# Expert pairs in alternating halves, a scatter that waits for the one two pairs ahead, and a reordered last pair

## The chip, the cores and the metric

The kernel runs on one core of a Trainium2 chip. The metric is the time of one execution on the device in microseconds (us); the profile gives beside it the span of the profiled execution, from its first to its last recorded event. Engines are called PE (TensorE), DVE (VectorE), ACT (ScalarE), POOL (GpSimd) and SP (SyncE); PEld is PE's loading of weights.

## The reference, cut to what matters

The whole is a transformer-like block of two parts on 512 tokens of width 1024. Only its last step is touched, a mixture of experts: 32 experts in 4 groups of 8; each token goes to one group and, in it, to its two best experts.

```python
g_sel = jnp.argmax(g_logits, axis=-1)
e_in = jnp.take_along_axis(e_logits, g_sel[:, None, None], axis=1)[:, 0]
top_v, top_i = lax.top_k(e_in, TOP_K_EXPERTS)
...
for g in range(N_GROUPS):
    a = jnp.einsum('nd,edf->nef', hf, w_gate[g])
    b = jnp.einsum('nd,edf->nef', hf, w_up[g])
    hid = jax.nn.silu(a) * b * gates[:, g, :, None].astype(hf.dtype)
    out = out + jnp.einsum('nef,efd->nd', hid, w_down[g])
```

So two experts of different groups never share a token, and two experts of one group often do. All is float32.

## The kernel before

**Pairs.** The experts are worked on in 16 pairs (`PAIRS`), each of the same expert number in two groups; 64 slots (`CAP`) for each expert, 128 rows in all. A list made from the routing (`listed`, columns of `ixg`) names the token of each slot; an empty slot names none and its row isn't moved. The order of the pairs is first all 8 of groups 0 and 1, then all 8 of groups 2 and 3 (`of_pairs`, and the same order in the arrays `w_gu` and `w_dn` that the host lays out). Neighbouring pairs are therefore of the same two groups.

**One pair u**, step by step:

1. POOL `gather(u)`: an indirect DMA fetches the pair's rows of `h_rows` (DRAM) into `hg[:, u % 2]` (`ex_rows` in the trace). It copies the list's column first (L2631) and issues at L2632.
2. PE `turn(u)` (L2721): 8 transposes of these rows. DVE `copy_rows(u)` (L2876, L2879) brings them into `hgT`.
3. PE `gate_up(u)` (L2734): 32 matmuls against two weight loads of 2 MB; after the first 16 `gu_half` counts, after all `gu_done`.
4. ACT `silu(u)` (L2841), DVE `hidden(u)` (L2886).
5. PE `turn_hidden(u)` (L2744), DVE `copy_hidden(u)` (L2891).
6. PE `down(u)` (L2757): 16 matmuls against one weight load of 2 MB, 8 into each of two banks of PSUM.
7. ACT `copy_y(u)` (L2846) and DVE `copy_y(u)` (L2896) bring one bank each into `ys[:, u % 2]`.
8. POOL `scatter(u)`: copies the list's column (L2639), waits for the two copies (L2641, L2643) and issues an indirect DMA that adds the rows to `out` (L2644).
9. POOL `y_is_out` (L2650, L2651): waits until a scatter has landed and gives its half of `ys` free (`y_free`).

**Order on PE.** The loop of `first_round` interleaves three pairs:

```python
for u in range(PAIRS):
    gate_up_first(u)
    if u + 1 < PAIRS:
        turn(u + 1, (u + 1) % 2, 16 * ((u + 1) // 2 + 1))
    if u:
        down_first(u - 1)
    turn_hidden(u, u % 2)
```

**Order on POOL.** Gathers and scatters are issued by one instruction stream that stands still at each wait, and both move on one DMA queue, q0 in the profile. Three gathers stand ahead, then `scatter(0)`, then a loop over `step`: gather, wait for the scatter of the pair before, scatter, and the same for the other half of the buffers. Since the scatters add to the same DRAM rows, no scatter is issued before the last one has landed.

**Weights.** SP loads 48 parts of 2 MB (`PARTS`: two of gate and up, one of down for each pair) through 11 places in SBUF, in the order in which PE uses them; a part is issued when the one 11 ahead has been used. They move on queue q1. The first 11 are loaded while the routing is worked out.

If an expert has more than 64 tokens, further rounds follow; with these inputs they don't run.

Of the kernel before, what the change touches and what calls it, by code (L numbers as in the profile page):

```python
# [15 lines left out]
ALU = mybir.AluOpType  # L16
# [5 lines left out]
P = 128  # L22
# [120 lines left out]
class Core:  # L143


    def __init__(self, nc, ctx, dram):
        self.nc, self.ctx, self.dram = nc, ctx, dram
        self.names = 0
        self.scope, self.held = ExitStack(), []
        self.W = ctx.enter_context(nc.sbuf_tensor("weight_slots", [P, SLOTS, KT * P], F32))  # L150
        self.w_in = [ctx.enter_context(nc.semaphore(f"weight_slot_{j}")) for j in range(SLOTS)]
        self.w_n = [0] * SLOTS

        self.place_in = [ctx.enter_context(nc.semaphore(f"place_in_{i}")) for i in range(PLACES)]

    def sem(self, name):
# [73 lines left out]
    def load_down(self, sp, i, pair):  # L230
        src = self.dram["w_dn"][bass.ds(pair, 1)].rearrange("x p c -> p (x c)").rearrange("p (s c) -> p s c", c=KT * P)
        sp.dma_start(self.place(i), src).then_inc(self.place_in[i], 16)

    def load_part(self, sp, c):

        kind, u, h = PARTS[c]
        if kind == "g":
            self.load_gate_up(sp, c % PLACES, u, h)
        else:
            self.load_down(sp, c % PLACES, u)  # L240

# [2049 lines left out]
def routing_programs(core, lot, omT, x_rows, gate, most, ixg, hg, hg_in, out):  # L2291
# [58 lines left out]
    def tensor(pe):  # L2350
# [40 lines left out]
        for j in range(2 * NB):  # L2391
            for x in range(2):
                units = of_pairs(unit_id[:, j], x)
                last = nc.tensor.matmul(pL[CAP * x:CAP * x + CAP, 0:PAIRS], at_slot[:, j], units, start=(j == 0),
                                        stop=(j == 2 * NB - 1))
        last.then_inc(listed, 1)
        pe.wait_ge(spread_rs, 2)
        for kind, table in enumerate((unit_one, unit_id)):
            for j in range(2 * NB):
                for x in range(2):  # L2400
                    last = nc.tensor.matmul(pz[CAP * x:CAP * x + CAP, kind * PAIRS:(kind + 1) * PAIRS], at_slot[:, j],  # L2401
                                            of_pairs(table[:, j], x), start=(j == 0), stop=(j == 2 * NB - 1))
        last.then_inc(listed_rs, 1)

# [160 lines left out]
def expert_programs(core, lot, most, ixg, hg, hg_in, out):  # L2565
# [10 lines left out]
    ix_ready, gu_half, gu_done, silu_done, th_done, d_done, more_spread, more_listed, more_ready = (  # L2576
        core.sem(n) for n in ("ix_ready", "gate_up_half", "gate_up", "silu", "hidden_turned", "down", "spread_rounds",
                              "listed_rounds", "rounds_ready"))
    t_done, ta_out, tb_out, hid_done, hT_done, ya, yb = (
        lot.t_done, lot.ta_out, lot.tb_out, lot.hid_done, lot.hT_done, lot.ya, lot.yb)  # L2580
# [44 lines left out]
    def gpsimd(pool):  # L2625
# [22 lines left out]

        def y_is_out(e, value):
            pool.wait_ge(y_out[e], value)  # L2650
            nc.gpsimd.tensor_tensor(ixc[:, 6:7], ixc[:, 2 + e:3 + e], ixc[:, 2 + e:3 + e], ALU.add).then_inc(y_free, 1)  # L2651

        def step(u, stored, ahead):
            if ahead:
# [10 lines left out]
            scatter(u + 1, 0)  # L2665
            chain.restart()

        def first_round():
            gather(1, 1)
            gather(2, 0)  # L2670
            gather(3, 1)
            pool.wait_ge(lot.x_stored, 16)
            scatter(0, 0)
            chain.restart()
            with pool.Fori(0, PAIRS // 2 - 2) as i:
                step(pool.snap(i * 2 + 1), pool.snap(i * 16 + 16), True)
            step(PAIRS - 3, first_out - 16, False)
            y_is_out(0, first_out)
            pool.wait_ge(y_free, PAIRS + 1)
            scatter(PAIRS - 1, 1)  # L2680
            chain.restart()

        def run(r):
            first, n = r * PAIRS, PAIRS
# [29 lines left out]
    def tensor(pe):  # L2714
# [31 lines left out]
            last.then_inc(th_done, 1)  # L2746

        def down(u, e, at, w):
            pe.wait_ge(place_in[at], w)
            pe.wait_ge(hT_done, u + 2)  # L2750
            pe.wait_ge(ya, u + 1)
            pe.wait_ge(yb, u + 1)
            for half in range(2):
                for f in range(FF // P):
                    for x in range(2):
                        rows = slice(CAP * x, CAP * x + CAP)
                        last = nc.tensor.matmul(pY[rows, half, :], hidT[:, e, f * P + CAP * x:f * P + CAP * x + CAP],  # L2757
                                                core.as_down(at)[:, x, f, half * 512:half * 512 + 512], start=(f == 0),
                                                stop=(f == FF // P - 1))
            last.then_inc(d_done, 1)  # L2760

        def filled_first(c):
            return 16 * (c // PLACES + 1)
# [7 lines left out]
            down(u, u % 2, c % PLACES, filled_first(c))  # L2771

        def first_round():
            for u in range(PAIRS):
                gate_up_first(u)
                if u + 1 < PAIRS:
                    turn(u + 1, (u + 1) % 2, 16 * ((u + 1) // 2 + 1))
                if u:
                    down_first(u - 1)
                turn_hidden(u, u % 2)  # L2780
            down_first(PAIRS - 1)

        def list_rounds():

            pe.wait_ge(more_spread, 2)
            for n, what in enumerate((slot_id, slot_rs, at_slot)):
                for j in range(2 * NB):
                    for x in range(2):
                        units = of_pairs(at_unit[:, j], x)
                        last = nc.tensor.matmul(pL[CAP * x:CAP * x + CAP, n * (MORE // 2):(n + 1) * (MORE // 2)], what[:, j],  # L2790
                                                units, start=(j == 0), stop=(j == 2 * NB - 1))
            last.then_inc(more_listed, 1)

# [43 lines left out]
    def scalar(act):  # L2837
# [3 lines left out]
            nc.scalar.activation(sa[:, e], pG[:, e, 0:FF], ACT.Silu, scale=rs2[:, e, 0:1]).then_inc(silu_done, 1)  # L2841

        def copy_y(u, e):
            act.wait_ge(d_done, u + 1)
            act.wait_ge(y_free, u + 1)
            nc.scalar.copy(ys[:, e, 0:512], pY[:, 0, :]).then_inc(ya, 1)  # L2846

# [20 lines left out]
    def vector(dve):  # L2868
# [29 lines left out]
        def run(r):  # L2898
            first, n = r * PAIRS, PAIRS
            hidden(first, 0)  # L2900
            copy_rows(first + 1, 1)
            copy_hidden(first, 0)
            with dve.Fori(0, n // 2 - 1) as i:
                u = dve.snap(i * 2 + (first + 1))
                hidden(u, 1)
                copy_rows(u + 1, 0)
                copy_y(u - 1, 0)
                copy_hidden(u, 1)
                hidden(u + 1, 0)
# [4 lines left out]
            hidden(u, 1)  # L2914
            copy_y(u - 1, 0)
            copy_hidden(u, 1)
            copy_y(u, 1)
            if not isinstance(r, int):
                copy_rows(u + 1, 0)
# [163 lines left out]
def layout(inputs):  # L3083
# [28 lines left out]
    arr["w_gu"] = np.ascontiguousarray(gu.reshape(2, 2, EPG, 2, KT // 2, P, 2 * FF).transpose(0, 2, 5, 3, 1, 4, 6)).reshape(  # L3112
        PAIRS, P, 2, -1)
    arr["w_dn"] = np.ascontiguousarray(dw.reshape(2, 2, EPG, FF // P, P, D).transpose(0, 2, 4, 1, 3, 5)).reshape(PAIRS, P, -1)
# [63 lines left out]
```

## Time and profile before

| | |
|---|---|
| three runs | 1533.16, 1533.18 and 1535.5 us, median 1533.18 |
| the profiled execution | 1533.7 us, its span 1531.9 us, mean granted clock 0.982 |
| busy in the span | PE 1418.7 us, DVE 820.9, ACT 418.4, POOL 56.4 |
| the experts | from the first gather at 1280.5 us to the end |

In rows of a timeline the columns are start and duration in us, engine, line of the kernel, operation, output and inputs, shapes and count; in brackets how long the engine was idle before it and what ended that. A duration of a matmul group covers its whole count. In rows of the chain they are start, duration and what the time went to. In windows: the stretch and its length, then the busy time of each engine with its number of instructions, the granted clock of PE (1.00 is 2.4 GHz, 0.50 is 1.2 GHz), the busy share of the 16 DMA engines and GB/s.

### The profile page before, as it was taken

What the parts mean: (1) busy time and instruction counts of PE and PEld (TensorE: products, weight loads), DVE (VectorE), ACT (ScalarE), POOL (GpSimd) and SP (SyncE); (2) the same over time, 40 slices, a digit from 0 to 9 for tenths busy, and PEclk for the clock granted to TensorE, in tenths of its full rate; (3) what the DMA queues carried; (4) which work ended last, traced back from release to release, by engine and by line L of the source; (5) the groups of instructions that cost most, each with busy time, mean ns of one, the idle gap of its engine ahead of it and who ended that gap; (6) DMA issues with size and microseconds to landing.
All of it is one profiled execution on the core that took longest, in us unless ns stands there. A gap on an engine that the chain in (4) does not pass through costs nothing. (4 is left out here: it accounts for less than half of the span.)

```text
span 1531.9 us, 14470 instructions
## 1 busy us (share of the span) xinstructions
PE 1418.7 (93%) x5162; PEld 760.5 (50%) x5162; DVE 820.9 (54%) x1808; ACT 418.4 (27%) x682; POOL 56.4 (4%) x114
## 2 busy tenths in 40 slices
PE   7999999999999999999989999998899795989875
PEld 3455555555555558888854344445444433333321
DVE  5567677676776847776443348965333414211210
ACT  2434444443345315101110133134301430000000
POOL 0000000000000000000000000000000001122211
PEclk9999999999999999999999999999999996999998
DMA  7131111321110114222342121002023468999994
GB/s 283 29 109 55 51 46 42 100 66 55 55 42 28 42 53 154 83 83 83 111 164 79 39 82 55 28 9 83 28 71 143 167 253 341 402 407 407 411 404 131
DMA packets 38056, 201.94 MB, mean 132 GB/s; under 512 B 6880, under 2 KB 8800, under 8 KB 31072
## 3 DMA queue, kind: packets, MB, share of 16 engines
q1 hardware_dynamic: 30688, 186.29, 32.4%
q0 software_dynamic: 4608, 8.40, 2.3%
q10 hardware_dynamic: 2688, 6.29, 1.1%
q8 instruction: 44, 0.72, 0.2%
q14 instruction: 28, 0.23, 0.0%
HBM read 196.77 MB, written 12.58 MB: 137 GB/s over the span
## 5 line engine op out<-in xcount | busy, mean ns | idle before, releaser
L446 PE MATMUL gla_proj<-hT,weight_slots 128*128 128x512 f32 x864 | 378.1, 592 | 1.9 <-DVE hT L809 1.9
L446 PEld LDWEIGHTS gla_proj<-hT,weight_slots 128*128 128x128 f32 x864 | 160.9, 190 | 188.8 <-issue 188.1
L2734 PE MATMUL moe_banks<-weight_slots,moe_room 128*64 128x512 f32 x400 | 91.4, 605 | 12.6 <-DMA weight_slots<-in_w_gu 9.7
L1503 PE MATMUL mid_p_proj<-hT,weight_slots 128*128 128x512 f32 x208 | 94.7, 603 | 2.4 <-DVE hT L1671 2.4
L2886 DVE SCALAR_TENSOR_TENSOR moe_room<-moe_banks,moe_kept,moe_room 128x256 f32<-128x256 f32 x16 | 7.7, 484 | 125.8 <-ACT moe_room L2841 118.8
L600 ACT ACTIVATE gla_level_decay<-gla_level_decay 128x1024 f32<-128x1024 f32 x56 | 59.0, 1057 | 39.4 <-DVE gla_level_decay L729 39.0
L1503 PEld LDWEIGHTS mid_p_proj<-hT,weight_slots 128*128 128x128 f32 x208 | 39.7, 193 | 53.9 <-issue 52.8
L2734 PEld LDWEIGHTS moe_banks<-weight_slots,moe_room 128*64 128x64 f32 x400 | 29.0, 139 | 66.6 <-issue 53.1
L1328 PE MATMUL rn_p_out<-mT,weight_slots 128*128 128x512 f32 x128 | 58.4, 618 | 3.4 <-PEq L949 3.4
L472 PEld LDWEIGHTS gla_level<-gla_level_q,gla_level_k 128*128 128x128 f32 x448 | 55.0, 192 | 11.5 <-issue 11.5
L564 ACT COPY gla_raw<-gla_proj 128x512 f32<-128x512 f32 x38 | 22.4, 590 | 130.6 <-PE gla_proj L446 130.6
L1328 PE MATMUL rn_p_out<-y2T,weight_slots 128*128 128x512 f32 x128 | 55.2, 593 | 1.5 <-PEq L170 1.5
L472 PE MATMUL gla_level<-gla_level_q,gla_level_k 128*128 128x128 f32 x448 | 56.3, 275 | 0.0
L446 PE MATMUL gla_proj<-weight_slots,hT 128*128 128x512 f32 x128 | 55.9, 592 | 0.0
L2451 POOL DMA_INDIRECT ex_rows<-h_rows,ix_rows x1 | 1.2, 1187 | 1280.1 <-issue 1280.1
L745 DVE COPY spare<-spare 128x1 f32<-128x1 f32 x64 | 9.6, 150 | 71.7 <-PE gla_level L472 71.1
L746 DVE COPY_PREDICATED gla_scores<-gla_level_masks,gla_level 128x512 f32<-128x512 int32 x64 | 46.8, 731 | 2.2
L2757 PE MATMUL moe_banks<-weight_slots,moe_room 128*64 128x512 f32 x176 | 41.9, 619 | 5.4 <-DMA weight_slots<-in_w_dn 4.6
L2841 ACT ACTIVATE moe_room<-moe_banks,moe_kept 128x256 f32<-128x256 f32 x16 | 7.6, 474 | 133.3 <-PE moe_banks L2734 133.3
L1328 PEld LDWEIGHTS rn_p_out<-mT,weight_slots 128*128 128x128 f32 x128 | 25.3, 199 | 35.4 <-issue 35.4
L1328 PEld LDWEIGHTS rn_p_out<-y2T,weight_slots 128*128 128x128 f32 x128 | 24.2, 190 | 31.8 <-issue 31.8
L446 PEld LDWEIGHTS gla_proj<-weight_slots,hT 128*128 128x128 f32 x128 | 23.9, 190 | 28.2 <-issue 28.2
(453 smaller groups left out, 2310.5 us busy)
## 6 DMA issues: line engine op xcount, KB each, us to landing
weight_slots<-in_w_gu SPq DMA_DIRECT2D x25, 2048.0 KB, 27.6
weight_slots<-in_w_dn SPq DMA_DIRECT2D x11, 2048.0 KB, 37.8
weight_slots<-in_w_gla SPq DMA_DIRECT2D x40, 512.0 KB, 3.6
weight_slots<-in_w_merge SPq DMA_DIRECT2D x32, 512.0 KB, 4.2
weight_slots<-in_w_out SPq DMA_DIRECT2D x16, 512.0 KB, 4.1
weight_slots<-in_w_v SPq DMA_DIRECT2D x3, 2048.0 KB, 7.8
hT<-in_w_gu SPq DMA_DIRECT2D x3, 2048.0 KB, 37.0
weight_slots<-in_w_u SPq DMA_DIRECT2D x8, 512.0 KB, 5.9
```

Of the source, the lines that this page charges most:

```text
L446: last = nc.tensor.matmul(pj[:, n % 2, :], lhsT, rhs, start=(k == 0), stop=(k == KT - 1))
L472: last = nc.tensor.matmul(pA[:, l % 2, c * P:(c + 1) * P], k, q, start=True, stop=True)
L564: nc.scalar.copy(dst, pj[:, n % 2, :]).then_inc(evac, 1)
L600: nc.scalar.activation(Tl[:, l % 2], Tl[:, l % 2], ACT.Exp).then_inc(e_ready, 1)
L745: chain(nc.vector.tensor_copy(core.spare[:, 1:2], core.spare[:, 0:1]))
L746: nc.vector.copy_predicated(A[:], masks[:, l].unsqueeze(1).to_broadcast([P, NB, P]), pA[:, l % 2].rearrange("p (n t) -> p n t", t=P)).then ...
L1328: last = nc.tensor.matmul(pp[:, j, :], core.slot(j)[:, k, :], src[:, k, :], start=(k == 0), stop=(k == KT - 1))
L1503: last = nc.tensor.matmul(pw[:, n % 2, :], a, b, start=(k == 0), stop=(k == KT - 1))
L2734: last = nc.tensor.matmul(pG[rows, e, :], hgT[:, k, rows], core.as_gate_up(at[k // 4])[:, x, k % 4, :], start=(k == 0), stop=(k == KT - 1))
L2757: last = nc.tensor.matmul(pY[rows, half, :], hidT[:, e, f * P + CAP * x:f * P + CAP * x + CAP], core.as_down(at)[:, x, f, half * 512:half ...
L2841: nc.scalar.activation(sa[:, e], pG[:, e, 0:FF], ACT.Silu, scale=rs2[:, e, 0:1]).then_inc(silu_done, 1)
L2886: nc.vector.scalar_tensor_tensor(out=hid[:, e], in0=pG[:, e, FF:2 * FF], scalar=rs2[:, e, 1:2], in1=sa[:, e], op0=ALU.mult, op1=ALU.mult). ...
```

## The change

It has six parts. (`step` stays as it is, for the further rounds; the last hunk of the diff is ACT's.)

1. `of_pairs`, `in_pairs` and the two host arrays: the pairs now alternate, pair 0 of groups 0 and 1, pair 1 of groups 2 and 3, and so on. Neighbouring pairs have no token in common.
2. `step_first` and `first_round` on POOL: a scatter waits only for the one two pairs ahead. `scatter(1)` stands directly behind `scatter(0)` and ahead of the loop, and the loop's scatters are one pair further on than its gathers were.
3. `down` gives two signals, `d_half` after the first bank and `d_done` after the second; ACT copies the first bank after `d_half`. Each half waits for its own bank to be free.
4. On PE `turn_hidden(15)` moves ahead of `down(14)`; on DVE `copy_hidden(15)` moves ahead of `copy_y(14)`.
5. The last weights (down of pair 15) come in two loads of 1 MB, by columns; the first half of `down(15)` waits for the first alone.
6. `y_is_out` reads the other index column.

```diff
 def of_pairs(units, x):
-    return units.rearrange("p (g x m) -> p x g m", x=2, m=EPG)[:, x]
+    return units.rearrange("p (r y x m) -> p x r m y", y=2, x=2, m=EPG)[:, x]
+def in_pairs(units):
+    return units.rearrange("p (r m y) -> p r m y", y=2, m=EPG)
...
+    def load_down_halves(self, sp, i, pair):
+        src = self.dram["w_dn"][pair].rearrange("p (x f c) -> p x f c", x=2, c=D)
+        for half, loaded in enumerate((self.last_half, self.place_in[i])):
+            cols = slice(half * 512, half * 512 + 512)
+            sp.dma_start(self.as_down(i)[:, :, :, cols], src[:, :, :, cols]).then_inc(loaded, 16)
...
         def y_is_out(e, value):
             pool.wait_ge(y_out[e], value)
-            nc.gpsimd.tensor_tensor(ixc[:, 6:7], ixc[:, 2 + e:3 + e], ixc[:, 2 + e:3 + e], ALU.add).then_inc(y_free, 1)
+            other = ixc[:, 3 - e:4 - e]
+            nc.gpsimd.tensor_tensor(ixc[:, 6:7], other, other, ALU.add).then_inc(y_free, 1)
 
         def step(u, stored, ahead):
             if ahead:
                 gather(u + 3, 0)
             y_is_out(0, stored)
             if not ahead:
                 pool.wait_ge(y_free, u + 2)
             scatter(u, 1)
             if ahead:
                 gather(u + 4, 1)
             y_is_out(1, stored)
             if not ahead:
                 pool.wait_ge(y_free, u + 3)
             scatter(u + 1, 0)
             chain.restart()
+        def step_first(u, stored, ahead):
+            if ahead:
+                gather(u + 3, 0)
+            y_is_out(0, stored)
+            if not ahead:
+                pool.wait_ge(y_free, u + 2)
+            scatter(u + 1, 0)
+            if ahead:
+                gather(u + 4, 1)
+            y_is_out(1, stored)
+            if not ahead:
+                pool.wait_ge(y_free, u + 3)
+            scatter(u + 2, 1)
+            chain.restart()
         def first_round():
             gather(1, 1)
             gather(2, 0)
             gather(3, 1)
             pool.wait_ge(lot.x_stored, 16)
             scatter(0, 0)
+            scatter(1, 1)
             chain.restart()
             with pool.Fori(0, PAIRS // 2 - 2) as i:
-                step(pool.snap(i * 2 + 1), pool.snap(i * 16 + 16), True)
-            step(PAIRS - 3, first_out - 16, False)
+                step_first(pool.snap(i * 2 + 1), pool.snap(i * 16 + 16), True)
+            step_first(PAIRS - 3, first_out - 16, False)
             y_is_out(0, first_out)
-            pool.wait_ge(y_free, PAIRS + 1)
-            scatter(PAIRS - 1, 1)
-            chain.restart()
...
         def down(u, e, at, w):
-            pe.wait_ge(place_in[at], w)
             pe.wait_ge(hT_done, u + 2)
-            pe.wait_ge(ya, u + 1)
-            pe.wait_ge(yb, u + 1)
             for half in range(2):
+                if half or isinstance(u, int) and u == PAIRS - 1:
+                    pe.wait_ge(place_in[at] if half else core.last_half, w if half else 16)
+                else:
+                    pe.wait_ge(place_in[at], w)
+                pe.wait_ge((ya, yb)[half], u + 1)
...
-            last.then_inc(d_done, 1)
+                last.then_inc((d_half, d_done)[half], 1)
...
         def first_round():
-            for u in range(PAIRS):
+            for u in range(PAIRS - 1):
                 gate_up_first(u)
-                if u + 1 < PAIRS:
-                    turn(u + 1, (u + 1) % 2, 16 * ((u + 1) // 2 + 1))
+                turn(u + 1, (u + 1) % 2, 16 * ((u + 1) // 2 + 1))
                 if u:
                     down_first(u - 1)
                 turn_hidden(u, u % 2)
+            gate_up_first(PAIRS - 1)
+            turn_hidden(PAIRS - 1, (PAIRS - 1) % 2)
+            down_first(PAIRS - 2)
             down_first(PAIRS - 1)
...
         def copy_y(u, e):
-            act.wait_ge(d_done, u + 1)
+            act.wait_ge(d_half, u + 1)
```

**How the order moves on POOL.** Around the entry to the loop, the kernel before has `gather(3)`, `scatter(0)`, then the loop's first piece, `gather(4)`:

```order
L2632 DMA ex_rows<-h_rows,ex_ix 128x1024
L2639 COPY ex_ix<-ix_rows 128x1
L2641 ISA
L2641 TENSOR_TENSOR ex_ix<-ex_ix 128x1
L2643 TENSOR_TENSOR ex_ix<-ex_ix 128x1
L2644 DMA out<-moe_room,ex_ix 512x1024
L134 ISA
L2675 UNCONDITIONAL_BRANCH
L2675 ISA
L2631 ISA
L2631 COPY ex_ix<-ix_rows 128x1
L2632 DMA ex_rows<-h_rows,ex_ix 128x1024
```

The changed kernel, at the same place, from the end of `scatter(0)` to `gather(4)` (its lines are some 15 further on):

```order
L2658 TENSOR_TENSOR ex_ix<-ex_ix 128x1
L2659 DMA out<-moe_room,ex_ix 512x1024
L2654 COPY ex_ix<-ix_rows 128x1
L2656 TENSOR_TENSOR ex_ix<-ex_ix 128x1
L2658 TENSOR_TENSOR ex_ix<-ex_ix 128x1
L2659 DMA out<-moe_room,ex_ix 512x1024
L134 ISA
L2707 UNCONDITIONAL_BRANCH
L2707 ISA
L2646 ISA
L2646 COPY ex_ix<-ix_rows 128x1
L2647 DMA ex_rows<-h_rows,ex_ix 128x1024
```

`gather(4)` stood behind one scatter and stands behind two; as the loop keeps this distance, every gather from the fourth on moves from behind `scatter(u - 4)` to behind `scatter(u - 3)`.

**On PE**, the end of the experts; before, from `turn_hidden(14)` and `gate_up(15)` on:

```order
L2744 MATMUL moe_banks<-ident,moe_room 128x128 x2
L2734 MATMUL moe_banks<-weight_slots,moe_room 64x512 x16
L2757 MATMUL moe_banks<-weight_slots,moe_room 64x512 x8
L2744 MATMUL moe_banks<-ident,moe_room 128x128 x2
L2757 MATMUL moe_banks<-weight_slots,moe_room 64x512 x8
```

And in the changed kernel, from `down(13)` on:

```order
L2788 MATMUL moe_banks<-x_rows,moe_room 64x512 x8
L2773 MATMUL moe_banks<-ident,moe_room 128x128 x2
L2763 MATMUL moe_banks<-weight_slots,moe_room 64x512 x16
L2773 MATMUL moe_banks<-ident,moe_room 128x128 x2
L2788 MATMUL moe_banks<-weight_slots,moe_room 64x512 x16
```

The second `turn_hidden` (that of pair 15) has moved ahead of `down(14)`, so that the two last `down` stand together.

## Rows read from the trace of the kernel before

**Rows 1.** The page, DMA queues: packets, MB, share of 16 engines' span.
```profile
q0 software_dynamic: 4608, 8.40, 2.3%
```

**Rows 2.** Windows of the experts' stage, 100 us each.
```profile
1300.00:1400.00 100.00, 92.45 (x438) 33.85 (x438) 20.88 (x44) 7.42 (x14) 24.56 (x48) 0.98 1.01 406
1400.00:1500.00 100.00, 80.10 (x384) 29.11 (x384) 20.06 (x42) 7.42 (x14) 22.87 (x46) 1.00 1.00 404
```

**Rows 3.** Waits, 1290 to 1532 us: who for whom, total, times, longest.
```profile
POOL ex_ix L2651 <- DMA out<-moe_room,ex_ix: 130.7, 15, 11.0
```

**Rows 4.** Timeline of POOL: scatters 0, 1, 13, 15 and gathers 4, 5.
```profile
1313.94 1.61 POOL L2644 DMA_INDIRECT out<-moe_room,ex_ix  x1 [0.53 <-remote]
...
1316.55 1.07 POOL L2632 DMA_INDIRECT ex_rows<-h_rows,ex_ix  x1 [0.79 <-POOL ex_ix L2631]
1326.85 0.19 POOL L2651 TENSOR_TENSOR ex_ix<-ex_ix 128x1 int32<-128x1 int32 x1 [9.23 <-DMA out<-moe_room,ex_ix]
...
1328.15 1.60 POOL L2644 DMA_INDIRECT out<-moe_room,ex_ix  x1 [0.47 <-issue]
...
1330.72 1.08 POOL L2632 DMA_INDIRECT ex_rows<-h_rows,ex_ix  x1 [0.77 <-POOL ex_ix L2631]
...
1498.81 1.59 POOL L2644 DMA_INDIRECT out<-moe_room,ex_ix  x1 [0.46 <-issue]
...
1524.00 1.58 POOL L2644 DMA_INDIRECT out<-moe_room,ex_ix  x1 [0.37 <-POOL ex_ix L2639]
```

**Rows 5.** Timeline of PE and DVE: down 1, 5, 13, turns 4 and 7, others.
```profile
1320.63 3.65 PE L2757 MATMUL moe_banks<-xT,moe_room 128*64 128x512 f32 x16
...
1332.89 1.09 PE L2721 MATMUL moe_banks<-ident,ex_rows 128*128 128x128 f32 x8 [1.22 <-DMA ex_rows<-h_rows,ex_ix]
...
1337.86 7.09 PE L2734 MATMUL moe_banks<-weight_slots,moe_room 128*64 128x512 f32 x32
...
1374.81 1.97 PE L2721 MATMUL moe_banks<-ident,ex_rows 128*128 128x128 f32 x8 [2.49 <-DMA ex_rows<-h_rows,ex_ix]
1376.70 4.30 PE L2757 MATMUL moe_banks<-hT,moe_room 128*64 128x512 f32 x16
...
1493.58 3.65 PE L2757 MATMUL moe_banks<-x_rows,moe_room 128*64 128x512 f32 x16 [1.48 <-DMA x_rows<-in_w_dn]
...
1503.32 3.65 PE L2734 MATMUL moe_banks<-weight_slots,moe_room 128*64 128x512 f32 x16 [1.10 <-DMA weight_slots<-in_w_gu]
...
1507.53 0.48 DVE L2886 SCALAR_TENSOR_TENSOR moe_room<-moe_banks,moe_kept,moe_room 128x256 f32<-128x256 f32 x1 [9.22 <-ACT moe_room L2841]
```

**Rows 6.** The chain of waits, around 1386 us and at the end.
```profile
1386.17 15.89 DMA ex_rows<-h_rows,ex_ix
1402.11 1.09 PE moe_banks L2721 x8
1403.20 3.58 PE moe_banks L2757 x16
...
1510.12 5.38 PE moe_banks L2757 x16
...
1517.01 5.69 DMA out<-moe_room,ex_ix
```

**Rows 7.** Tiles `ex_rows` (the gathers), then `out` (the scatters): issue to landing.
```profile
DMA to landing us min/median/max: 8.0/15.1/16.1
...
DMA to landing us min/median/max: 5.7/12.4/13.0
```

**Rows 8.** Timeline of SP: weight loads issued around `gate_up(3)`.
```profile
1324.32 0.33 SPq L228 DMA_DIRECT2D xT<-in_w_gu  x1
...
1331.71 0.33 SPq L228 DMA_DIRECT2D weight_slots<-in_w_gu  x1
```

**Rows 9.** Windows of 2 us behind PE's wait at 1372 to 1375 us.
```profile
1376.00:1378.00 2.00, 2.00 (x8) 0.90 (x8) 1.08 (x3) 0.00 (x0) 0.00 (x0) 0.50 1.07 373
1378.00:1380.00 2.00, 2.00 (x12) 0.58 (x10) 0.28 (x1) 0.00 (x0) 0.00 (x0) 0.99 1.01 400
```

More of the change, by code:

```diff
@@ L152, in __init__ @@
         self.w_n = [0] * SLOTS
+        self.last_half = ctx.enter_context(nc.semaphore("last_down_half"))
         self.place_in = [ctx.enter_context(nc.semaphore(f"place_in_{i}")) for i in range(PLACES)]
@@ L238, in load_part @@
             self.load_gate_up(sp, c % PLACES, u, h)
+        elif u == PAIRS - 1:
+            self.load_down_halves(sp, c % PLACES, u)
         else:
@@ L2393, in tensor @@
                 units = of_pairs(unit_id[:, j], x)
-                last = nc.tensor.matmul(pL[CAP * x:CAP * x + CAP, 0:PAIRS], at_slot[:, j], units, start=(j == 0),
+                last = nc.tensor.matmul(in_pairs(pL[CAP * x:CAP * x + CAP, 0:PAIRS]), at_slot[:, j], units, start=(j == 0),
                                         stop=(j == 2 * NB - 1))
@@ L2400, in tensor @@
                 for x in range(2):
-                    last = nc.tensor.matmul(pz[CAP * x:CAP * x + CAP, kind * PAIRS:(kind + 1) * PAIRS], at_slot[:, j],
+                    last = nc.tensor.matmul(in_pairs(pz[CAP * x:CAP * x + CAP, kind * PAIRS:(kind + 1) * PAIRS]), at_slot[:, j],
                                             of_pairs(table[:, j], x), start=(j == 0), stop=(j == 2 * NB - 1))
@@ L2575, in expert_programs @@
     y_out, y_free = lot.y_out, lot.y_free
-    ix_ready, gu_half, gu_done, silu_done, th_done, d_done, more_spread, more_listed, more_ready = (
-        core.sem(n) for n in ("ix_ready", "gate_up_half", "gate_up", "silu", "hidden_turned", "down", "spread_rounds",
+    ix_ready, gu_half, gu_done, silu_done, th_done, d_half, d_done, more_spread, more_listed, more_ready = (
+        core.sem(n) for n in ("ix_ready", "gate_up_half", "gate_up", "silu", "hidden_turned", "down_half", "down", "spread_rounds",
                               "listed_rounds", "rounds_ready"))
@@ L2789, in list_rounds @@
                         units = of_pairs(at_unit[:, j], x)
-                        last = nc.tensor.matmul(pL[CAP * x:CAP * x + CAP, n * (MORE // 2):(n + 1) * (MORE // 2)], what[:, j],
+                        last = nc.tensor.matmul(in_pairs(pL[CAP * x:CAP * x + CAP, n * (MORE // 2):(n + 1) * (MORE // 2)]), what[:, j],
                                                 units, start=(j == 0), stop=(j == 2 * NB - 1))
@@ L2914, in run @@
             hidden(u, 1)
+            copy_hidden(u, 1)
             copy_y(u - 1, 0)
-            copy_hidden(u, 1)
             copy_y(u, 1)
@@ L3111, in layout @@
     gu = np.concatenate([gw.reshape(EXPERTS, KT, P, FF), uw.reshape(EXPERTS, KT, P, FF)], 3)
-    arr["w_gu"] = np.ascontiguousarray(gu.reshape(2, 2, EPG, 2, KT // 2, P, 2 * FF).transpose(0, 2, 5, 3, 1, 4, 6)).reshape(
+    arr["w_gu"] = np.ascontiguousarray(gu.reshape(2, 2, EPG, 2, KT // 2, P, 2 * FF).transpose(2, 0, 5, 3, 1, 4, 6)).reshape(
         PAIRS, P, 2, -1)
-    arr["w_dn"] = np.ascontiguousarray(dw.reshape(2, 2, EPG, FF // P, P, D).transpose(0, 2, 4, 1, 3, 5)).reshape(PAIRS, P, -1)
+    arr["w_dn"] = np.ascontiguousarray(dw.reshape(2, 2, EPG, FF // P, P, D).transpose(2, 0, 4, 1, 3, 5)).reshape(PAIRS, P, -1)
     arr["w_xo"] = _tiles(a["xattn_wo_2"][0])
```

## The prediction

> **What bounds the experts' stage now.** The change lies wholly in it. I first read the windows: from 1300 to 1500 us the DMA engines are busy all the time, at 406 and 404 GB/s, while PE falls from 92% to 80% [rows 2]. So the stage is as long as its transfers, if nothing makes PE use the places later. Then the waits: POOL's largest one, 130.7 us in 15 times, is for the scatter before [rows 3]; that is the wait that the change loosens. Does it cost time? I followed POOL's stream [rows 4]: scatter 0 goes out at 1313.94, gather 4 behind it at 1316.55 (2.6 us later), the landing is noticed at 1326.85, scatter 1 goes out at 1328.15, 14.2 us after scatter 0. And PE does wait for gathers: turn 4 at 1332.89 and turn 7 at 1374.81 [rows 5], and the chain around 1386 us runs through a gather of 15.89 us [rows 6]. From down 1 (end 1320.63 + 3.65 = 1324.28) to down 13 (end 1493.58 + 3.65 = 1497.23) the 12 steps take 173 us, 14.4 us each [rows 5].
>
> **The step on which all rests: where the gathers now stand.** Before, gather k+4 follows scatter k. Scatter k needs down k. Gather k+4 is needed by turn k+4, which stands on PE ahead of down k+2. So a round of the chain down → scatter → gather → turn → down spans two pairs. In the changed order gather k+3 follows scatter k: the prelude holds a second scatter and no further gather, and the loop keeps that distance. Turn k+3 stands ahead of down k+1. The same chain now spans one pair, and nothing on PE can pass it, since its stream is in order. The change in the scatters' wait frees nothing in this ring, since scatter k waits for down k anyhow.
>
> Price of one round, from rows of before:
> - end of a down to the issue of its scatter (copies of 0.6 to 0.7 us, and POOL's steps): 1497.23 to 1498.81, 1.6 us [rows 4, 5]
> - scatter's issue to the gather's: 2.6 us, twice [rows 4]
> - the gather's issue to landing: 8.0 least, 15.1 median, 16.1 most [rows 7]. I take 15.1: nearly all gathers of before stand directly behind a scatter, as all do now.
> - landing to turn and down: 1402.11 to 1403.20 + 3.58, 4.7 us, and 0.1 to start
> - the clock: after PE's wait ahead of 1374.81 the granted clock was 0.50 (1.2 GHz) until about 1378 [rows 9], and turn and down took from 1374.81 to 1376.70 + 4.30 = 1381.00, 6.2 us instead of 4.7. PE would now stand still for some 10 us in each round (25.5 less turn, down, turn_hidden and 7.1 us of gate_up), longer than there, so I add these 1.5 us each time.
>
> Sum: 1.6 + 2.6 + 15.1 + 0.1 + 4.7 + 1.5 = 25.6 us for each pair, against 14.4 us.
>
> Does the queue of weights leave the gathers as slow as now? The stage moves 6 MB (6.3 million bytes) for each pair; at 406 GB/s [rows 2] that is 15.5 us, so in 25.6 us it would be idle for 10. But its loads are issued as places are used: one as down k ends (1324.32), the last at the end of the gate_up behind it (1331.71) [rows 8]. They keep the queue full from about 1 us to some 17 us after the end of down k; the gather is out from 4.2 to 19.3 us. It lies within nearly all of that. So I keep 15.1 and let the idle time fall behind it.
>
> **The whole.** Down 1 ends at 1324.28 as before: turns 1 to 3 have their gathers from the prelude. Scatter 1 goes out at 1325.9 (before 1328.15), gather 4 at 1328.5, landing 1343.6, turn 4 and down 2 end at 1349.9 (0.1 + 4.7 + 1.5). Gathers 5 to 15 give 11 more rounds: down 13 ends at 1349.9 + 11 × 25.6 = 1631.5. Then turn_hidden 14 (0.4), gate_up 15 (7.1 [rows 5]): 1639.0. Its product is ready about 1.0 us after (before: 1506.97 to 1507.53 + 0.48 [rows 5]), turn_hidden 15 takes 0.5 with its start: 1640.5. Down 14 and down 15, back to back with weights long there, 3.6 us each: 1647.7. Scatter 15 at +1.6: 1649.3. In the profiled run of before scatter 15 went out at 1524.00 [rows 4] and the span ended at 1531.9, 7.9 us later: span 1657.2, and with the 1.8 us around the span (1533.7 less 1531.9) 1659 us. The median of before is 1533.18, 0.5 less than the profiled run: about **1658 us**, 8% slower.
>
> **The other parts of the change** are small and lie at the end. The order of pairs moves no work: the same 1024 rows (8.40 MB of q0 [rows 1] for gathers and scatters together), in another order; zero. `d_half` lets ACT copy 1.8 us earlier (half of 3.65), but the scatter waits for DVE's copy behind the second half; zero in the ring. The second wait inside `down` is long satisfied when the bank's copy is an idle period away; if not, it costs up to the copy's 0.7 us, once a pair, inside the range. The moved turn_hidden and the two 1 MB loads serve a wait for the last weights; with a weight queue that idles 10 us in each round these weights are there, so they bring nothing but the order I summed above. The scatter of pair 15 no longer waits for that of pair 14: in the present tail it would bring the 3.3 us worked out below.
>
> **A rule that speaks for the change.** Rows 7 hold no gather under 8.0 us; one moves 8.40 MB / 32 = 0.26 MB [rows 1, 7]. The Trainium skill (DMA: Bandwidth & Descriptors, "Anatomy of one DMA — SWDGE (gpsimd) path") gives a fit of 2.0 us plus the bytes over 436 GB/s for a DMA of this kind. By it a gather would be an estimated 2.6 us; the trace disagrees (15.1 us median [rows 7], weights moving beside it). The nearest row on that side is the shortest scatter, 5.7 us, at the end with no weights left [rows 6, 7].
>
> **The rivals.**
> - *The gathers are off the path and only the tail is left* (faster). It takes a gather that lands within 14.4 − 1.6 − 2.6 − 0.1 − 4.7 = 5.4 us. The least of 16 is 8.0, the least scatter 5.7. If so: down 14 ends at 1510.12 + 5.38 = 1515.50 [rows 6], down 15 follows at once (3.6, to 1519.1), scatter 15 goes out at 1520.7 instead of 1524.00: 3.3 us less, 1530 us; 1528 if the clock stays up. By the fit of the Trainium skill quoted above, this is what would come. Chance 0.03.
> - *The weight queue drains early and the gathers land in 8 to 10 us* (slower, but by far less). Mechanism: PE is late, so places come free late and the DMA engines are free when the gather comes. Round 1.6 + 2.6 + 8.0 + 0.1 + 4.7 = 17.0 without a loss of clock; 12 rounds are 12 × 8.6 = 103 us less than my sum: 1555; with 10 us and the clock's 1.5 it is 20.5, and 1597. For it: 10 idle us in each round. Against it: the times of issue in [rows 8]. Chance 0.10.
> - *Nothing shows*: turn k+3 late, but the transfers bound the stage anyhow. It takes a round of at most 14.4 us too, as in the first rival. Chance 0.01.
> - *The forecast*, rounds of 21 to 27 us: chance 0.86.
>
> **Range.** With the gather at 16.1 each round is 26.6 us, 1670; with turn and down wholly at 0.50 (twice 4.7 instead of 6.2) 28.8, 1696. With a gather of 11 us, halfway from the least to the median, 21.5, 1609. I give 1600 to 1685. A measurement of this kernel tells about 0.2% (3 us) from no change; slower by over 0.2% are forecast and second rival.
>
> **What the profile after would show.** Right: POOL's L2647 (the gather) out 4.2 us after each down; turns 4 to 15 each with a wait for `ex_rows` of about 10 us on PE; downs 24 to 27 us apart; DMA share about 0.6 to 0.7 in the windows where it was 1.00; the granted clock falling in each round; POOL's wait for landed scatters nearly gone, and nothing gained by it; the weights of pair 15 no wait. Wrong in size: gathers that land in 8 to 10 us, which [rows 8] should then have shown in when loads are issued. Wrong at all: turns with no wait for `ex_rows` and downs 14 us apart. Then I would have misread which gather stands behind which scatter.

## The result and the profile after

The changed kernel takes 1629.74 us (median of four runs, 1629.29 to 1635.06), the kernel before 1533.17 (four runs, 1532.66 to 1535.5). The ratio is 1.0639, with a 95% interval of 1.0625 to 1.0653: 6.4% slower. The profiled execution took 1629.83 us, its span is 1628.0, the mean granted clock 0.950.

The windows of the changed kernel over the experts' stage, with the columns of [rows 2] and a third stretch, which before did not have:

```profile
1300.00:1400.00 100.00, 65.42 (x288) 24.60 (x284) 13.29 (x28) 5.29 (x10) 13.49 (x28) 0.83 0.84 335
1400.00:1500.00 100.00, 55.30 (x228) 21.12 (x228) 11.45 (x24) 3.75 (x8) 14.22 (x27) 0.76 0.70 273
1500.00:1600.00 100.00, 65.84 (x285) 24.28 (x283) 13.23 (x29) 5.19 (x10) 18.02 (x35) 0.83 0.60 216
```

Where the DMA engines were busy all the time at 406 and 404 GB/s, they are now busy 84, 70 and 60% of it. PE fell from 92 and 80% to between 55 and 66%, and its clock from 0.98 and 1.00 to 0.76 to 0.83. So the transfers no longer set the pace. The waits from 1290 us to the end say what does (who for whom and for what, total us, times, longest):

```profile
POOL ex_ix L2656 <- ACT moe_room L2879: 226.8, 16, 20.2
...
PE moe_banks L2750 <- DMA ex_rows<-h_rows,ex_ix: 113.4, 12, 12.3
...
POOL ex_ix L2667 <- DMA out<-moe_room,ex_ix: 1.3, 1, 1.3
```

POOL's wait for landed scatters has gone from 130.7 us in 15 times [rows 3] to 1.3 us in one. In its place POOL waits 226.8 us for ACT's copies behind the first half of `down`, and PE 113.4 us in 12 times for the gathers. The wait that the change set out to remove is removed, and the kernel is 97 us slower. POOL's timeline, scatters 0 and 1 and gather 4, then scatters 14 and 15:

```profile
1312.93 1.61 POOL L2659 DMA_INDIRECT out<-moe_room,ex_ix  x1 [0.63 <-issue]
...
1324.85 1.59 POOL L2659 DMA_INDIRECT out<-moe_room,ex_ix  x1 [0.55 <-remote]
...
1327.45 1.08 POOL L2647 DMA_INDIRECT ex_rows<-h_rows,ex_ix  x1 [0.82 <-POOL ex_ix L2646]
...
1617.20 1.59 POOL L2659 DMA_INDIRECT out<-moe_room,ex_ix  x1 [0.52 <-issue]
...
1620.64 1.57 POOL L2659 DMA_INDIRECT out<-moe_room,ex_ix  x1 [0.47 <-POOL ex_ix L2654]
```

Gather 4 went out at 1316.55 before [rows 4]. It now goes out at 1327.45, behind `scatter(1)`. The other side of it is on PE's timeline: `down(1)`, turn 4, turn 8 with the `down(6)` behind it, turns 13, 14 and 15, `down(13)`.

```profile
1319.64 3.65 PE L2788 MATMUL moe_banks<-xT,moe_room 128*64 128x512 f32 x16
...
1342.10 1.97 PE L2750 MATMUL moe_banks<-ident,ex_rows 128*128 128x128 f32 x8 [11.43 <-DMA ex_rows<-h_rows,ex_ix]
...
1442.56 1.97 PE L2750 MATMUL moe_banks<-ident,ex_rows 128*128 128x128 f32 x8 [11.04 <-DMA ex_rows<-h_rows,ex_ix]
1444.46 5.64 PE L2788 MATMUL moe_banks<-weight_slots,moe_room 128*64 128x512 f32 x16
...
1568.98 1.97 PE L2750 MATMUL moe_banks<-ident,ex_rows 128*128 128x128 f32 x8 [9.20 <-DMA ex_rows<-h_rows,ex_ix]
...
1585.44 1.09 PE L2750 MATMUL moe_banks<-ident,ex_rows 128*128 128x128 f32 x8 [1.60 <-DMA ex_rows<-h_rows,ex_ix]
...
1598.49 1.09 PE L2750 MATMUL moe_banks<-ident,ex_rows 128*128 128x128 f32 x8 [0.99 <-DMA ex_rows<-h_rows,ex_ix]
1599.52 3.65 PE L2788 MATMUL moe_banks<-x_rows,moe_room 128*64 128x512 f32 x16
```

From turn 4 to turn 13 nine rounds take 1568.98 − 1342.10 = 226.9 us, 25.2 us each. The last two take 16.5 and 13.1 us. The chain shows one round whole, from the issue of gather 8 to that of gather 9, and then the gathers of the last two rounds:

```profile
1428.31 14.21 DMA ex_rows<-h_rows,ex_ix
1442.56 1.97 PE moe_banks L2750 x8
1444.53 3.64 PE moe_banks L2788 x8
1448.19 0.59 ACT moe_room L2879
...
1451.63 1.61 POOL out L2659
...
1454.26 14.77 DMA ex_rows<-h_rows,ex_ix
...
1580.63 4.77 DMA ex_rows<-h_rows,ex_ix
...
1594.29 4.16 DMA ex_rows<-h_rows,ex_ix
```

Down → scatter → gather → turn → down, with nothing beside it: that is the ring, a closed chain of waits in which each round starts only when the last has ended. It reads: gather 14 us, turn and `down` 7.5 us, most of it at the lower clock, 1.5 us to the scatter, 2.6 us to the next gather.

### The profile page after: what moved, and what is told of

Same layout as the page of the kernel before. It is cut to its first block and busy times, and to the rows that moved or that the text cites. A ratio compares the mean times of both kernels' runs of the same rounds, so it can differ in the third digit from the quotient of the medians.

```text
span 1628.0 us, 14471 instructions
## 1 busy us (share of the span) xinstructions
PE 1434.7 (88%) x5162; PEld 768.6 (47%) x5162; DVE 820.5 (50%) x1808; ACT 418.2 (26%) x682; POOL 57.5 (4%) x114
## 3 DMA queue, kind: packets, MB, share of 16 engines
q0 software_dynamic: 4608, 8.40, 2.3%
## 5 line engine op out<-in xcount | busy, mean ns | idle before, releaser
L2750 PE MATMUL moe_banks<-ident,ex_rows 128*128 128x128 f32 x128 | 27.1, 381 | 113.4 <-DMA ex_rows<-h_rows,ex_ix 113.4
L2763 PE MATMUL moe_banks<-weight_slots,moe_room 128*64 128x512 f32 x400 | 90.4, 603 | 2.9 <-DVE moe_room L2912 2.9
L2750 PEld LDWEIGHTS moe_banks<-ident,ex_rows 128*128 128x128 f32 x128 | 21.5, 197 | 126.5 <-DMA ex_rows<-h_rows,ex_ix 124.0
L2919 DVE SCALAR_TENSOR_TENSOR moe_room<-moe_banks,moe_kept,moe_room 128x256 f32<-128x256 f32 x16 | 7.7, 484 | 113.4 <-ACT moe_room L2874 113.4
L574 ACT COPY gla_raw<-gla_proj 128x512 f32<-128x512 f32 x38 | 22.4, 590 | 130.7 <-PE gla_proj L456 130.7
L2879 ACT COPY moe_room<-moe_banks 128x512 f32<-128x512 f32 x16 | 9.4, 585 | 176.5 <-PE moe_banks L2788 172.0
L2788 PE MATMUL moe_banks<-weight_slots,moe_room 128*64 128x512 f32 x176 | 51.2, 737 | 0.0
## 6 DMA issues: line engine op xcount, KB each, us to landing
weight_slots<-in_w_gu SPq DMA_DIRECT2D x25, 2048.0 KB, 11.8
```

The source lines that it names most:

```text
L574: nc.scalar.copy(dst, pj[:, n % 2, :]).then_inc(evac, 1)
L2750: last = nc.tensor.transpose(pT[:, k // 4, (k % 4) * P:(k % 4 + 1) * P], hg[:, e, k * P:(k + 1) * P], core.ident[:])
L2763: last = nc.tensor.matmul(pG[rows, e, :], hgT[:, k, rows], core.as_gate_up(at[k // 4])[:, x, k % 4, :], start=(k == 0), stop=(k == KT - 1))
```

## The experiments

The numbers of pairs and of turns are the kernel's own: turn k belongs to pair k, and `down(k)` stands on PE behind turn k + 2. The kernels ran on three chips, on each beside the kernel before: late_gathers, gathers_back, old_pool and no_weights on the first (kernel before 1533.20 us, median of 19 runs), catch_up, gather_first, one_load and old_turn on the second (1533.02, 27 runs), gathers_back_2 and old_turn_2 on the third (1532.59, 23 runs). A ratio is that of an experiment to the kernel before on its chip, with a 95% interval. Some diffs are shortened; the text then says what they leave out.

**late_gathers: the position of the gathers alone.** It is the kernel before, with nothing changed but that the gathers stand one scatter later; pairs, waits, signals and loads are those of before. The diff shows the loop's piece for the first round against `step`.

```diff
-            if ahead:
-                gather(u + 3, 0)
             y_is_out(0, stored)
             scatter(u, 1)
+            if ahead:
+                gather(u + 3, 0)
-            if ahead:
-                gather(u + 4, 1)
             y_is_out(1, stored)
             scatter(u + 1, 0)
+            if ahead:
+                gather(u + 4, 1)
```

> The kernel before with one edit: in the first round each gather k+3 is issued behind scatter k, as in the changed kernel; every wait, the pair order and the tail are those of before. Theory (the ring: down k, scatter k, gather k+3, turn k+3, down k+1): rounds of about 25 us while weights are loaded, two of about 13.5 us at the end, 1630 to 1635 us in all, as the changed kernel has 1630 plus its tail of 3 us. Rival A (two scatters in flight load the queue and slow the gathers): here only one scatter is in flight, so 1533 to 1560 us. Rival B (the pair order or the half waits in down cost it): 1533 us.

Measured: 1640.29 us (1638.61 to 1643.22, four runs), ratio 1.0705 (1.0689 to 1.072). PE's turns 4 and 13:

```profile
1347.24 1.97 PE L2736 MATMUL moe_banks<-ident,ex_rows 128*128 128x128 f32 x8 [14.98 <-DMA ex_rows<-h_rows,ex_ix]
...
1577.35 1.97 PE L2736 MATMUL moe_banks<-ident,ex_rows 128*128 128x128 f32 x8 [13.08 <-DMA ex_rows<-h_rows,ex_ix]
```

Nine rounds in 230.1 us, 25.6 us each. The whole loss comes with the moved gathers; neither the looser wait nor any of the other five parts is needed for it. Here too the last two rounds are short. The time is 5 to 10 us above what I expected, and the trace says where it goes: turn 4 is 5.1 us later than in the changed kernel, since scatter 1 still waits for scatter 0's landing (3.7 us later), the nine rounds take 3.2 us more, and the strict waits of the tail are there too.

**gathers_back: everything but that.** The changed kernel, with each gather put back behind the scatter that it followed before.

```diff
             scatter(0, 0)
+            gather(4, 0)
             scatter(1, 1)
...
-                gather(u + 3, 0)
+                gather(u + 4, 1)
             y_is_out(0, stored)
             scatter(u + 1, 0)
-                gather(u + 4, 1)
+                gather(u + 5, 0)
             y_is_out(1, stored)
             scatter(u + 2, 1)
```

> The changed kernel with the gathers at the distance of before (gather k+4 behind scatter k), and all else of the change. Theory: the ring spans two pairs again, the downs are 13 to 15 us apart, the weights bound the stage as before, and only the tail is left of the change: 1527 to 1531 us. Rival A (two scatters in flight): still well over 1550 us, since the scatters wait as loosely as in the changed kernel. Rival B (pair order, half waits): also well over 1550 us.

Measured: 1527.38 us (1525.78 to 1531.38, eight runs), ratio 0.9971 (0.996 to 0.9983); run again on a third chip (gathers_back_2) 1529.69 us (1526.91 to 1530.79, 11 runs), ratio 0.9983 (0.9974 to 0.9992).

> The run gathers_back again, on one chip with the next, to tell small parts apart. It had 1527.4 us against 1533.2 before (ratio 0.997). Theory: the loosened scatter wait gives about 4 to 6 us at the tail, 1527 to 1529 us. Rival: the first job flattered it and it is at 1530 to 1533.

The windows, turns 6 and 8, and the last two scatters:

```profile
1300.00:1400.00 100.00, 97.52 (x474) 35.45 (x472) 22.92 (x48) 8.47 (x16) 27.10 (x52) 1.00 1.01 404
1400.00:1500.00 100.00, 79.24 (x352) 28.52 (x348) 17.19 (x36) 6.35 (x12) 20.54 (x41) 0.95 1.00 403
```

```profile
1355.28 1.09 PE L2752 MATMUL moe_banks<-ident,ex_rows 128*128 128x128 f32 x8 [0.85 <-DMA ex_rows<-h_rows,ex_ix]
...
1379.86 1.09 PE L2752 MATMUL moe_banks<-ident,ex_rows 128*128 128x128 f32 x8 [0.53 <-DMA ex_rows<-h_rows,ex_ix]
```

```profile
1512.82 1.58 POOL L2659 DMA_INDIRECT out<-moe_room,ex_ix  x1 [0.52 <-issue]
...
1516.47 1.58 POOL L2659 DMA_INDIRECT out<-moe_room,ex_ix  x1 [0.52 <-POOL ex_ix L2654]
```

The DMA share is back at 1.00: the transfers bound the stage again. PE is freed early in it (97.5% against 92.5% in [rows 2]) and waits for weights later. What remains is a shorter end: scatter 15 goes out 3.65 us behind scatter 14, where it was 7.0 before (1524.00 less 1517.01, [rows 4, 6]). The ring is still there, but it now spans two pairs: turns 6 and 8 both wait for their gathers and stand 24.6 us apart. This is the version that beats both kernels, by 3 to 6 us over the one before. The repetition, 1529.7 us, lies just above the 1527 to 1529 expected for it. Part of the spread stands ahead of the change's reach: turn 3 begins at 1317.22 in one profiled execution and at 1320.01 in the other. From turn 3 to the end of the span it is 206.8 and 209.0 us, and 212.3 in the kernel before (turn 3 at 1319.60), so 3.3 to 5.5 us less.

**old_pool: the order of the pairs, the half signals, the moved turn and the two loads, without the looser wait.** The changed kernel with POOL's whole stream of before.

```diff
-            other = ixc[:, 3 - e:4 - e]
...
             scatter(0, 0)
-            scatter(1, 1)
...
-                step_first(pool.snap(i * 2 + 1), pool.snap(i * 16 + 16), True)
-            step_first(PAIRS - 3, first_out - 16, False)
+                step(pool.snap(i * 2 + 1), pool.snap(i * 16 + 16), True)
+            step(PAIRS - 3, first_out - 16, False)
             y_is_out(0, first_out)
+            pool.wait_ge(y_free, PAIRS + 1)
+            scatter(PAIRS - 1, 1)
```

> The changed kernel with POOL's stream of before (each scatter waits for the one before, gathers at their old distance); pair order, half signals, moved turn_hidden and last weights in two loads stay. Theory: the middle is that of before. The last scatter still waits for the one before it; down 15 ends up to 3 us earlier, so 1530 to 1533 us. Rival B (pair order or half waits cost it): over 1550 us.

Measured: 1533.21 us (1529.55 to 1535.4, 11 runs), ratio 0.9997 (0.9988 to 1.0006). POOL's timeline at its end, scatter 14, the wait for its landing, scatter 15:

```profile
1518.97 1.58 POOL L2659 DMA_INDIRECT out<-moe_room,ex_ix  x1 [0.53 <-remote]
1524.88 0.19 POOL L2666 TENSOR_TENSOR ex_ix<-ex_ix 128x1 int32<-128x1 int32 x1 [4.33 <-DMA out<-moe_room,ex_ix]
...
1526.11 1.58 POOL L2659 DMA_INDIRECT out<-moe_room,ex_ix  x1 [0.38 <-POOL ex_ix L2654]
```

By themselves, with the strict wait in place, these four parts bring nothing that can be measured, not even the up to 3 us that I expected from an earlier `down(15)`; here the two last scatters are 7.1 us apart. Between this kernel and gathers_back, on the same chip, lie 5.8 us, and only POOL's stream, with the looser wait, stands between them.

**no_weights: is it the weights that make the gathers slow?** The changed kernel, without any weight load after the first 11 parts, so the pairs behind them compute with old weights.

```diff
         def first_round():
-            for c in range(PLACES, len(PARTS)):
...
+            return
...
         def filled_first(c):
-            return 16 * (c // PLACES + 1)
+            return 16
```

PE's waits for weights are thus met by the first filling of each place.

> The changed kernel without the weight loads past the first 11 parts (later pairs are computed with the weights that stand in the places). Theory: the ring stays, but a gather with no weights beside it lands in 4 to 5 us instead of 13.7: rounds of 1.6 + 2.6 + 4.5 + 0.1 + 4.7 = 13.5 us, with no fall of the clock; from down 1 to down 13 some 162 us, span about 1513 us. Rival (the last two rounds of the changed kernel were short for another reason, fewer rows in their pairs): rounds stay near 25 us.

Measured: 1506.07 us (one run). Its turns 7 and 9, and the gathers' time from issue to landing:

```profile
1368.24 1.09 PE L2747 MATMUL moe_banks<-ident,ex_rows 128*128 128x128 f32 x8 [0.44 <-DMA ex_rows<-h_rows,ex_ix]
...
1394.82 1.09 PE L2747 MATMUL moe_banks<-ident,ex_rows 128*128 128x128 f32 x8 [1.47 <-DMA ex_rows<-h_rows,ex_ix]
```

```profile
DMA to landing us min/median/max: 3.3/4.2/4.7
```

The same chain in the same order takes 26.6 us for two rounds, 13.3 us each (13.2 from turn 4 to turn 15), and the gathers land in 4.2 us instead of 14. So the ring of one pair costs little as such: about a microsecond a pair over the 12.0 at which PE goes where nothing waits (gather_first, below). It costs 25 us because a gather beside the weight queue takes over three times as long: that is 10 of the 12 us by which the rounds differ, and the lower clock behind the wait is the other 2. The span, 1504.3 us, is 9 us under the expected 1513; half of that lies between `down(1)` and `down(13)`, 157.5 us instead of 162.

**catch_up: is a late round given back later?** gathers_back, with gathers 4 to 8 as late as in the changed kernel and the old distance from then on. `step_late` is the loop's piece of the changed kernel.

```diff
             scatter(0, 0)
-            gather(4, 0)
             scatter(1, 1)
             chain.restart()
-            with pool.Fori(0, PAIRS // 2 - 3) as i:
+            with pool.Fori(0, 2) as i:
+                step_late(pool.snap(i * 2 + 1), pool.snap(i * 16 + 16))
+            gather(8, 0)
+            chain.restart()
+            with pool.Fori(2, PAIRS // 2 - 3) as i:
```

> The changed kernel's order for gathers 4 to 7, then one gather more (8) behind scatter 5 and from there the distance of gathers_back. Theory: turns 4 to 8 are late, the rounds between their downs take about 25 us, the others 13 to 15. The lost time is less than 5 times 11 us, since the DMA engines go on loading ahead while PE waits (some 7 of the 25 us idle in each late round) and PE can then run at its own pace of 12 to 13 us for a while: 1562 to 1583 us. Rival (two scatters in flight or the pair order slow all rounds): all rounds long, 1630 us.

Measured: 1564.5 us (one run). Windows, first with the late rounds, then behind them:

```profile
1340.00:1440.00 100.00, 57.74 (x232) 21.59 (x232) 11.46 (x24) 4.24 (x8) 15.67 (x30) 0.77 0.74 289
1440.00:1540.00 100.00, 93.08 (x444) 34.23 (x446) 22.44 (x47) 8.01 (x15) 25.50 (x51) 0.96 0.93 364
```

Turn 8 comes at 1443.87, 64 us later than in gathers_back (1379.86), and the kernel ends 35 to 37 us later than that one. So some 28 us are given back: while PE stands still the weights run ahead of it, and PE then goes through the pairs in 12.0 to 13.6 us each until it meets them again. Five late rounds cost about 7 us each in the end. In the changed kernel no pair is left in which to catch up but the last two.

**gather_first: the gather ahead of its scatter.** gathers_back, with `gather(k + 4)` ahead of `scatter(k)`.

```diff
             gather(3, 1)
+            gather(4, 0)
             scatter(0, 0)
-            gather(4, 0)
+            gather(5, 1)
             scatter(1, 1)
```

The loop's gathers move one step forward in the same way.

> The run gathers_back with each gather k+4 ahead of scatter k, one step further forward (it still follows turn k+2, which frees its buffer). Theory: turns no longer wait for their gathers at all, but weights bound the stage, so the downs of the second half and the end stay: 1526 to 1528 us, the same as gathers_back within 2 us. Rival (the gather waits of 0.5 to 1.1 us there still count, each of some ten rounds): 1517 to 1522 us.

Measured: 1529.48 us (1527.92 to 1532.13, 11 runs), ratio 0.9983 (0.9974 to 0.9992). The gathers, and PE at the first place where it waits:

```profile
DMA to landing us min/median/max: 7.5/11.4/13.7
```

```profile
1411.63 5.30 PE L2766 MATMUL moe_banks<-xT,moe_room 128*64 128x512 f32 x16 [2.37 <-DMA xT<-in_w_gu]
```

Gathers 4 us faster, turns 12.0 us apart and none waiting for rows until 1403 us; then PE stands at weights, and the end is the same (1527.4 and 1529.7 us for gathers_back, on other chips). With the old distance the gathers do not set the end, and the queue of weights does.

**one_load and old_turn: the two edits at the end.** gathers_back with the last weights in one load, and gathers_back with `turn_hidden(15)` and `copy_hidden(15)` back behind `down(14)` and `copy_y(14)`.

```diff
-        elif u == PAIRS - 1:
-            self.load_down_halves(sp, c % PLACES, u)
...
-                if half or isinstance(u, int) and u == PAIRS - 1:
-                    pe.wait_ge(place_in[at] if half else core.last_half, w if half else 16)
-                else:
-                    pe.wait_ge(place_in[at], w)
+                pe.wait_ge(place_in[at], w)
```

```diff
             gate_up_first(PAIRS - 1)
-            turn_hidden(PAIRS - 1, (PAIRS - 1) % 2)
             down_first(PAIRS - 2)
+            turn_hidden(PAIRS - 1, (PAIRS - 1) % 2)
             down_first(PAIRS - 1)
...
+            copy_y(u - 1, 0)
             copy_hidden(u, 1)
-            copy_y(u - 1, 0)
```

> The run gathers_back (1527.4 us) with the last weights in one load again. Its tail shows down 14 and down 15 back to back in 7.29 us (twice 3.65), so the last weights were no wait there. Theory: the split is worth something only as long as down 15 stands right behind down 14 and the slowest DMA engine is still at its first half: down 15 would start up to 2 us later, 1527 to 1530 us. Rival: the split carries most of the 5.8 us that gathers_back gained over before, so 1532 to 1533 us.

> The run gathers_back with turn_hidden 15 and copy_hidden 15 back behind down 14 and its copy. Theory: down 15 waits again for the turn and its copy, 0.4 + 0.1 + 0.7 + 0.4 us and the start of PE, 1.2 to 1.5 us on the end of the last scatter: 1528.5 to 1529 us. Rival: it is hidden, 1527.4 us.

> The run old_turn again (turn_hidden 15 behind down 14), on the same chip as gathers_back_2. Theory: 1.2 to 1.5 us more than gathers_back_2. Rival: the same as it.

Measured: one_load 1529.44 us (1527.25 to 1531.61, 11 runs), ratio 0.9975 (0.9966 to 0.9984); old_turn 1530.67 us (1527.17 to 1533.36, 11 runs), ratio 0.9987 (0.9978 to 0.9996), and on the third chip, as old_turn_2, 1530.83 us (1528.83 to 1533.35, 12 runs), ratio 0.999 (0.9981 to 0.9999). The single load does not show: its ratio lies between the two of gathers_back. The old place of the turn is 1.1 us slower than gathers_back on the third chip, and the intervals of the ratios overlap. So the moved turn may be worth a microsecond, which these runs don't settle.

## Why the prediction was right

The sign, the place and the price of a round were right; the time came out 28 us lower than forecast, inside the range: a loss of 97 us where 125 were forecast. Step by step:

- **The ring of one pair** is shown: it stands in the chain, and it comes and goes with the position of the gathers alone (late_gathers, gathers_back).
- **The price of a round, 25.6 us forecast, is 25.2 us.** From the end of a down to the scatter 1.6 (1323.29 to 1324.85), as forecast. Scatter to gather 2.6, as forecast. The gather 14.3 in the mean of the ten long rounds (12.4 to 15.5 along the chain) instead of 15.1. Turn and down 6.1 to 7.6 us, 6.8 in the mean, instead of 6.2: the clock. The two errors nearly cancel, which is luck. PE's wait was put at "some 10 us", though the terms beside it leave 11.8; it was 9.2 to 12.3.
- **The number of such rounds was the mis-sized term.** "11 more rounds" behind turn 4 were nine; the last two took 16.5 and 13.1 us. In ends of `down` (1576.45, 1590.11, 1603.17) these are 26.7 us where 51.2 were forecast: 24.5 of the 28.3 us by which `down(13)` (1631.5 forecast, 1603.17 measured) came early. The ten rounds ahead of them, 253.2 us against 256, and the start, 1.0 us earlier, are the rest. The cause stands on SP's timeline and in the DMA share of three windows behind it:

```profile
1556.39 0.33 SPq L233 DMA_DIRECT2D weight_slots<-in_w_dn  x1
...
1559.82 1.35 SPq L240 DMA_DIRECT2D weight_slots<-in_w_dn  x2
```

```profile
1562.00:1572.00 10.00, 3.02 (x12) 2.07 (x14) 0.91 (x3) 0.00 (x0) 0.00 (x0) 0.63 0.97 378
1572.00:1582.00 10.00, 10.00 (x43) 3.04 (x42) 1.47 (x3) 0.58 (x1) 3.54 (x7) 0.86 0.24 40
1582.00:1592.00 10.00, 8.39 (x44) 3.13 (x42) 2.87 (x6) 1.06 (x2) 0.78 (x4) 1.00 0.13 31
```

  The last weights are issued at 1559.8, since SP is 11 parts ahead of PE, which is 3.7 pairs. They have moved by about 1572, and gathers 14 and 15, issued behind that, land in 4.8 and 4.2 us. The 11 places stand in the description of the kernel; that the weights therefore end so many parts ahead of the last gathers I did not carry through. late_gathers, with the same loads, has the same two short rounds, 14.9 and 13.0 us.
- **"They keep the queue full"** held for every round with a weight load in it, and so the second rival (gathers in 8 to 10 us) fell for ten rounds. For the last two its outcome came, and by more than it said, though for another reason: no weights were left to load. no_weights shows what that does: with no weights beside them the gathers take 3.3 to 4.7 us.
- **The fit of the Trainium skill** (DMA: Bandwidth & Descriptors, "Anatomy of one DMA — SWDGE (gpsimd) path"), an estimated 2.6 us for such a gather, is far from the 14 us here, and even with the weights gone 4.2 us were measured.
- **The tail behind `down(13)`**: 17.8 us to scatter 15 forecast, 17.5 measured (1603.17 to 1620.64); then 7.9 forecast, 7.4 measured. With the 28.3 us of the point on the rounds the span is 29.2 us under the 1657.2 forecast.
- **The first rival's mechanism is real and was hidden.** "In the present tail it would bring the 3.3 us": in gathers_back the two last scatters are 3.4 us closer (3.65 instead of 7.0), and the kernel is 5.8 us faster than before on one chip and 2.9 on another. Only the condition that I gave for it, a gather under 5.4 us, failed here.
- **The other parts at about zero**: shown by old_pool with the strict wait in place (0.9997, from 0.9988 to 1.0006). Without it, one_load and old_turn leave room for a microsecond or so. None was tried by itself inside the slow ring.
- **The lower end of the range** rests on a slip: halfway from 8.0 to 15.1 is 11.6, not 11, which gives 1616 us and not 1609. Neither verdict nor mechanism hangs on it.

The gain of the change was given up at one place, where `scatter(1)` was put ahead of the loop without moving `gather(4)` up with it. In the order of before a round of the same length spans two pairs (24.6 us in gathers_back, 12.3 for each), and that hides beneath the weights, which set the 14.4 us; in the changed order it spans one.

## What to carry to other kernels

When instructions are moved by one turn of a loop on one engine, write down for each pair of them how many turns of the others' loops the ring between them now spans: a round's time over that number is the pace, whatever wait was removed. A small transfer on the path is to be priced as it lands beside the traffic of that moment, and where that traffic ends early the price falls with it, so count the rounds of each kind. If a prefetch must be late for a few rounds, keep some beyond them in which the rest can catch up.

## What the runs showed of the hardware

**A small gather beside a deep queue.** The same gather of 0.26 MB takes 3.3 to 4.7 us without weights moving and mostly 12 to 16 us with them. The two queues in 2 us of the kernel before (1459 to 1461; packets, MB, share of 16 engines):

```profile
q1 hardware_dynamic: 52, 0.80, 94.1%
q0 software_dynamic: 47, 0.03, 7.8%
```

Nearly as many packets move on q0 as on q1, but one of q1 is 0.80 MB / 52 = 15 KB and takes 0.941 × 32 / 52 = 0.58 us of an engine, while one of q0 takes 0.05 here. A few microseconds later, from 1468 to 1469, q0 is nearly out of work, and the counts part:

```profile
q1 hardware_dynamic: 33, 0.43, 99.7%
q0 software_dynamic: 3, 0.00, 1.1%
```

In no_weights, where q0 is alone, up to 93 of its packets move in one microsecond (1378 to 1379), against 18 to 32 beside the weights in the changed kernel (1330 to 1335). So while both have work, q0 gets on only as fast as the large packets of q1. The Trainium skill (DMA: Bandwidth & Descriptors, "Queues, rings and completion order") says that an engine takes turns between the queues that have work, a packet at a time; the equal counts agree. It puts several descriptors into a packet, and whether the profile counts packets in that sense no run here shows.

An estimate from rows: a scatter and the gather behind it are 2 × 144 packets (4608 for 32 transfers [rows 1]), 18 for each engine. One of q0 takes 2.3% × 16 × 1531.9 / 4608 = 0.12 us in the mean of the run [rows 1], so these are 18 × (0.58 + 0.12) = 12.6 us. From the scatter's issue to the gather's landing it is 2.6 + 14.2 = 16.8 us; what fills the other 4 us isn't shown. Smaller weight packets would put the account to a test, which wasn't made. gather_first agrees with the queue of the two: ahead of its scatter a gather takes 11.4 us (median), behind it 15.6 (gathers_back), and the scatter 13.8 instead of 12.3.

**The clock after a wait.** After each 9 to 12 us wait the turn takes 1.97 us instead of 1.09 and the `down` behind it 4.16 to 5.73 instead of 3.65. Windows of 2 us around turn 4 of the changed kernel:

```profile
1340.00:1342.00 2.00, 0.00 (x0) 0.00 (x0) 0.00 (x0) 0.00 (x0) 0.00 (x0) 0.50 0.99 418
...
1344.00:1346.00 2.00, 2.00 (x7) 0.77 (x8) 1.36 (x3) 0.00 (x0) 0.00 (x0) 0.50 0.99 426
1346.00:1348.00 2.00, 2.00 (x10) 0.57 (x9) 0.00 (x0) 0.58 (x1) 0.19 (x1) 0.98 0.88 377
```

The granted clock fell while PE stood still: it was 1.00 from 1332 to 1334 and 0.50 (1.2 GHz) from 1336 to 1338. It stayed at this lower level until about 1346, four microseconds into the work. That is 1.4 to 3.0 us more in each long round, 2.2 in the mean, on the ring; the one place of before that I sized it from had 1.5.
